# Attention operands split into high and low parts during the projection, head groups in the order B, C, A, and a full fp32 value product in group C

## The reference

```
h  = rmsnorm(x); z = h @ w_in                      # queries, keys, values of all three groups
A: 8 heads of 64, 2 key/value heads; q, k: rmsnorm per head, then a rotation (rope)
B: 4 heads; q = rmsnorm(cq) @ w_uq (64 + 32 rotated), k, v = rmsnorm(ckv) @ w_ukv,
   plus a rotated key kr of 32 that the four heads share
C: 4 heads with two maps of width 32 each: p_i = softmax(q_i k_i / sqrt(32) - slope * |distance|)
   a = p_0 - lam * p_1;  o = rmsnorm(a @ v)
x = x + concat(A, B, C) @ w_out
u = conv3(rmsnorm(x) @ w_up);  x = x + (silu(gate) * value) @ w_down        # width 2816
```

## Time and profile before

| | us |
|---|---|
| median of 3 runs | 3411.35 (3408.97 to 3412.27) |
| the profiled execution, its own time | 3407.34 |
| its span (first to last instruction) | 3405.5, mean granted clock 0.951 |
| PE busy in the span | 3034.8 (89%) |
| DVE, ACT, POOL busy | 2210.5 (65%), 1399.9 (41%), 825.5 (24%) |
| projection, layer 0 | from 42.8 to the first scores at 297.0 |
| attention, first transposes to the last unit | 310.7 to 857.8 |

### The profile page before, as it was taken

One profiled execution on the slowest core, in us unless ns is written; L12 is line 12 of the kernel. 1 busy time (PEld: TensorE's weight loads), 2 busy tenths in 40 slices (PEclk: granted clock), 3 DMA queues, 4 the chain that ended last, 5 costly groups with the idle time before them and its releaser, 6 DMA issues.

```text
span 3405.5 us, 41293 instructions
## 1 busy us (share of the span) xinstructions
PE 3034.8 (89%) x13488; PEld 2378.8 (70%) x13488; DVE 2210.5 (65%) x2575; ACT 1399.9 (41%) x1917; POOL 825.5 (24%) x472
## 2 busy tenths in 40 slices
PE   6888999666899999999889889995669999999996
PEld 5666777444678888888767667763447788888885
DVE  4863877899345656556567378779972556555555
ACT  3214888666232222222222178886643222222213
POOL 3113554653320000000121145555524100000002
PEclk8999999888999999999999999997789999999998
DMA  4323211210212112111133331111121112111112
GB/s 159 87 81 90 53 46 41 56 39 6 99 50 62 50 37 62 37 49 37 37 103 92 89 85 46 41 54 44 28 75 50 58 42 62 37 49 49 50 37 62
DMA packets 233562, 198.55 MB, mean 58 GB/s; under 512 B 49344, under 2 KB 207808, under 8 KB 233408
## 3 DMA queue, kind: packets, MB, share of 16 engines
q1 hardware_dynamic: 233408, 196.66, 20.1%
HBM read 163.07 MB, written 33.55 MB: 58 GB/s over the span
## 4 chain that ended last, share of the span: by engine, by line
PE 63%; DVE 15%; issue 13%; ACT 4%; DMA 2%; POOL 2%; DVEq 1%; ACTq 0%; SPq 0%; POOLq 0%
PE ps L1528 26%; PE ps L1542 13%; PE ps L1319 9%; PE ps L1417 5%; PE ps L1448 4%; DVE ps L1136 2%; DVE ptl L1178 2%; PE ps L1428 2%; PE ps L1429 2%; DVE r L1079 2%; PE ps L1513 1%; ACT prob L861 1%; PE ps L1460 1%; DVE rinv L1153 1%; ACT pth L891 1%
## 5 line engine op out<-in xcount | busy, mean ns | idle before, releaser
L574 POOL TENSOR_TENSOR w0l<-wraw,w0h 128x1024 fp32r<-128x1024 f32 x34 | 89.4, 2634 | 1692.7 <-ACT w0h L754 1692.7
L1448 PEld LDWEIGHTS ps<-cst,prob 128*128 128x128 f32 x2048 | 257.2, 148 | 272.2 <-DVE ptl L1178 141.9
L1448 PE MATMUL ps<-cst,prob 128*128 128x128 f32 x2048 | 336.3, 289 | 120.9 <-DVE ptl L1178 57.7
L1178 DVE TENSOR_TENSOR ptl<-ps,pth 128x512 fp32r<-128x512 f32 x512 | 349.0, 687 | 142.7 <-ACT pth L891 136.9
L1417 PE MATMUL ps<-stack 128*128 128x512 f32 (+1 forms) x1152 | 350.1, 426 | 96.6 <-ACT prob L861 77.0
L861 ACT ACTIVATE prob<-ps,nmx 128x1024 f32<-128x1024 f32 x320 | 356.7, 1115 | 83.7 <-DVE nmx L1140 63.6
L1257 DVE TENSOR_TENSOR xT<-ps,xT 128x512 f32<-128x512 f32 x352 | 242.4, 691 | 226.2 <-PE ps L1542 226.1
L891 ACT ACTIVATE pth<-ps 128x512 fp32r<-128x512 f32 x512 | 298.8, 595 | 192.6 <-PE ps L1448 188.7
L1417 PEld LDWEIGHTS ps<-stack 128*128 128x128 f32 (+1 forms) x1152 | 216.2, 199 | 180.9 <-ACT prob L861 115.4
L1319 PE MATMUL ps<-xgh,w0h 128*128 128x512 f32 x768 | 254.9, 414 | 49.9 <-DVE z L1049 15.1
L1542 PE MATMUL ps<-ah,dnh 128*128 128x512 f32 x704 | 276.3, 393 | 21.0 <-DVE dnl L1250 20.1
(11 more groups left out here) (183 smaller groups left out, 6088.1 us busy)
## 6 DMA issues: line engine op xcount, KB each, us to landing
wraw<-in_w_up SPq DMA_DIRECT2D x88, 512.0 KB, 4.6
draw<-in_w_down SPq DMA_DIRECT2D x22, 1024.0 KB, 5.0
wraw<-in_w_in SPq DMA_DIRECT2D x36, 512.0 KB, 4.5
x_d<-xT SPq DMA_DIRECT2D x2, 4096.0 KB, 15.8
raw<-qa_d SPq DMA_DIRECT2D x32, 256.0 KB, 3.8
raw<-ka_d SPq DMA_DIRECT2D x32, 256.0 KB, 4.2
vraw<-v_d SPq DMA_DIRECT2D x32, 256.0 KB, 3.1
wraw<-in_w_out SPq DMA_DIRECT2D x16, 512.0 KB, 5.0
```

Of the source, the lines that this page charges most:

```text
L1178: dve.tensor_tensor(ptl[:, s % NPT, :], ps[:, 4 + s % 2, :], pth[:, s % NPT, :].bitcast(F32), ALU.subtract).then_inc(pt_lo, 1)
L1448: ins = pe.transpose(ps[:, 4 + s % 2, m * P:(m + 1) * P], prob[:, b, m, s * P:(s + 1) * P], ident)
```

## The change

The stores of the projection now write high and low parts. After each tile or job ACT copies the high part into a ring of four slots (`hi_event`), DVE subtracts to get the low part (`lo_event`), and SP stores both (`store_event`); a ring slot pair is used again two events later, when its stores have landed (`ring_free`). A `z` slot is free with the low part. The DRAM arrays of A, B and C's operands and of A and B's values get a leading axis of two; C's values stay plain fp32. Attention loads the stacks directly (`load_operands`, `load_values`); `hi_operand`, `lo_operand`, `hi_values` and `lo_values` are gone, and so are the buffers `raw` and `vraw`.

The tiles alternate C and A, with A's key as tile 13. `uq` becomes three jobs of 128 rows (one of them all rotated parts, so there is one rotation in place of four; the host orders the columns of `w_uq`), and `tr` two jobs of 128 in place of four. The heads run in the order B, C, A; the units of B and C and one of A's are written out, and the loop runs over A. The operands of heads 0 and 1 are loaded during the projection, at tile 9.

In C the value product is one fp32 matmul a step (`vfull` with `ptf`) in place of the pair, `ptl` falls away, ACT copies the transposed probabilities unrounded, and DVE's `sum_output` scales the result itself; `copy_part` (ACT) and `scale_output` (POOL) do nothing there.

At the end of the FFN the last down weights go to slots of the up weights, so they can be split before group 9 is done; all 16 products of group 9 come after the last up products, and DVE interleaves its additions with taps, gate and splits (`last_step`).

```diff
-TILES += [("aq", A_Q + P * i) for i in range(4)] + [("ak", A_K)]
-TILES += [("cq_", C_Q), ("cq_", C_Q + P), ("ck_", C_K), ("ck_", C_K + P)]
-TILES += [("v", A_V), ("v", C_V), ("v", C_V + P)]
+TILES += [("cq_", C_Q), ("aq", A_Q), ("ck_", C_K), ("aq", A_Q + P), ("cq_", C_Q + P), ("aq", A_Q + 2 * P), ("ck_", C_K + P), ("aq", A_Q + 3 * P)]
+TILES += [("vc", C_V), ("ak", A_K), ("vc", C_V + P), ("va", A_V)]
...
-JOBS = {0: [("sx", 0)], 2: [("scq", 0)], 3: [("sckv", 0)], 4: [("uq", h) for h in range(4)],
-        5: [("sa", 4), ("ukv", 0), ("ukv", 1), ("tr", 0), ("ukv", 2), ("tr", 1), ("ukv", 3), ("tr", 2), ("tr", 3)],
-        6: [("sa", 5)], 7: [("sa", 6)], 8: [("sa", 7)], 9: [("sa", 8)],
-        14: [("tv", 13)], 15: [("tv", 14), ("tv", 15)]}
...
+JOBS = {0: [("sx", 0)], 2: [("scq", 0)], 3: [("sckv", 0)], 4: [("uq", 0), ("uq", 1), ("uq", 2)], 5: [("ukv", 0), ("ukv", 1)],
+        6: [("sa", 5), ("ukv", 2), ("ukv", 3)], 7: [("tr", 0), ("tr", 1)], 8: [("sa", 7)], 10: [("sa", 9)], 12: [("sa", 11)],
+        13: [("tv", 12)], 14: [("sa", 13)], 15: [("tv", 14), ("tv", 15)]}
...
+EVENTS = {4: [("z", 3), ("uq", 1), ("uq", 2), ("z", 4)], 5: [("uq", 0), ("ukv", 0), ("ukv", 1)], 6: [("z", 6), ("z", 5)], 7: [("tr", 0), ("tr", 1)],
+          8: [("z", 8), ("z", 7)], 10: [("z", 10), ("z", 9)], 12: [("z", 11)], 13: [("tv", 12)], 14: [("z", 13)], 15: [("tv", 14), ("tv", 15)]}
+EVENT_LIST = [e_ for t in range(NT) for e_ in EVENTS.get(t, [])]
+WHOLE = [("tv", 12), ("tv", 14)]
+SPLITS = [e_ for e_ in EVENT_LIST if e_ not in WHOLE]
...
-HEADS = [("A", h) for h in range(NA)] + [("B", h) for h in range(NB)] + [("C", h) for h in range(NC)]
+HEADS = [("B", h) for h in range(NB)] + [("C", h) for h in range(NC)] + [("A", h) for h in range(NA)]
...
+    qn_d, qr_d = dram("qn_d", (2, NB * NOPE, T)), dram("qr_d", (2, NB * ROPE, T))
+    kn_d, kr_d = dram("kn_d", (2, NB * NOPE, T)), dram("kr_d", (2, ROPE, T))
+    qc_d, kc_d = dram("qc_d", (2, NC * 2 * CQK, T)), dram("kc_d", (2, NC * 2 * CQK, T))
+    v_d, vc_d = dram("v_d", (2, T, (NKV + NB) * HD)), dram("vc_d", (T, NC * HD))
...
+                def store_event(kind, a):
...
+                    stored = ring_stored[n % 2]
+                    if (kind, a) in WHOLE:
...
+                    for s, ready in enumerate((split_hi, split_lo)):
+                        sp.wait_ge(ready, l * len(SPLITS) + split_no(kind, a))
+                        src = ring(kind, a, s).bitcast(F32)
...
+                            dst = {"aq": qa_d, "ak": ka_d, "cq_": qc_d, "ck_": kc_d}[name]
+                            sp.dma_start(dst[s, i * P:(i + 1) * P, :], src).then_inc(stored, 16)
...
+                def load_operands(hh):
+                    group, h = head(hh)
+                    st, full = stack[hh % 2], stack_full[hh % 2]
+                    if hh >= 2:
+                        sp.wait_ge(scores_done, l * NS + items_before(2 * hh - 2))
+                    if group == "A":
+                        for s in range(2):
...
                     else:
+                        for i in range(2):
+                            r0 = (2 * h + i) * CQK
+                            for c in range(4):
+                                rows = slice(c * CQK, (c + 1) * CQK)
+                                sp.dma_start(st[2 * i][rows, :].bitcast(F32), qc_d[c % 2, r0:r0 + CQK, :]).then_inc(full, 16)
+                                sp.dma_start(st[2 * i + 1][rows, :].bitcast(F32), kc_d[c // 2, r0:r0 + CQK, :]).then_inc(full, 16)
...
+                def load_values(hh):
+                    group, h = head(hh)
+                    full = v_full[hh % 2]
+                    if hh >= 2:
+                        sp.wait_ge(av_done, l * (8 * NU) + 16 * (hh - 1) + AV_CREDIT)
+                    if group == "C":
+                        sp.dma_start(vfull[hh % 2][:, :, :], vc_d.rearrange("(m p) c -> p m c", p=P)[:, :, h * HD:(h + 1) * HD]).then_inc(full, 16)
...
+                        load_operands(0)
+                        load_operands(1)
...
+                load_values(0)
+                load_values(1)
                 sp.dma_start(dtab[:, :], dist).then_inc(dtab_loaded, 16)
...
+                for hh in range(2, NB + NC + NA):
+                    load_operands(hh)
+                    load_values(hh)
...
-                def lo_operand(hh, i, s, h=None):
...
-                def hi_values(hh, h=None):
...
-                def lo_values(hh, h=None):
...
                 def scale_output(x):
...
+                    if x["group"] == "C":
+                        return
...
                 def pool_unit(x, prev, nx):
-                    hh, h = x["k"] // 2 + 1, x["hh"] + 1
-                    more = hh < NA + NB + NC
-                    ahead = operands_ahead(x)
-                    late = ahead and ahead[0] == "C"
                     diagonals(x)
-                    if ahead and not late:
-                        lo_operand(ahead[1], ahead[2], 0, ahead[3])
                     if nx and nx["group"] == "C":
                         mix_first(nx)
-                    if ahead:
-                        lo_operand(ahead[1], ahead[2], 0 if late else 1, ahead[3])
                     if prev:
                         scale_output(prev)
-                    if x["half"] == 1 and more:
-                        hi_values(hh, h)
-                    if late:
-                        lo_operand(ahead[1], ahead[2], 1, ahead[3])
-                    if x["half"] == 1 and more:
-                        lo_values(hh, h)
-                    if prev:
                         lo_mix(prev)
...
+                def ring_free(kind, a):
+                    n = event_no(kind, a)
+                    if n >= 2:
+                        act.wait_ge(ring_stored[n % 2], (l * RINGS[n % 2] + ring_dmas(n - 2)) * 16)
...
+                def hi_event(kind, a):
...
+                    act.activation(ring(kind, a, 0)[0:rows, :], src[0:rows, :], ACT.Copy).then_inc(split_hi, 1)
...
-                def hi_operand(hh, i, s, h=None):
...
                 def copy_part(x):
+                    if x["group"] == "C":
+                        return
...
-                        act.activation(pth[:, s % NPT, :], ps[:, 4 + s % 2, :], ACT.Copy).then_inc(pt_hi, 1)
+                        act.activation((ptf if x["group"] == "C" else pth)[:, s % NPT, :], ps[:, 4 + s % 2, :], ACT.Copy).then_inc(pt_hi, 1)
...
+                def lo_event(kind, a):
...
+                        src = e[:, 0, :] if kind == "uq" else z[:, a % 2, :]
+                        ins = dve.tensor_tensor(lo[0:rows, :], src[0:rows, :], hi[0:rows, :].bitcast(F32), ALU.subtract)
+                    ins.then_inc(split_lo, 1)
...
-                for h in range(NB):
-                    dve.wait_ge(job_free, l * NJ + job_no("uq", h) + 1)
-                    rope(e[:, h % 2, :], rb_, NOPE, 96, 8).then_inc(roped, 1)
-                    dve.wait_ge(roped, l * NB + h + 1)
+                for kind, a in EVENTS[4]:
+                    lo_event(kind, a)
+                dve.wait_ge(job_free, l * len(FREED) + free_no("uq", 0))
+                rope(e[:, 0, :], rb_, 0, P, 8).then_inc(roped, 1)
+                dve.wait_ge(roped, l + 1)
...
                 def sum_output(x):
-                    dve.wait_ge(part_copied, l * NU + x["u"] + 1)
+                    if x["group"] == "C":
+                        dve.wait_ge(av_done, l * (8 * NU) + x["u"] * 8 + 8 + AV_CREDIT)
+                        dve.wait_ge(norm_copied, l * NU + x["u"] + 1 + N_CREDIT)
+                        dve.wait_ge(mix_lo, l * NU + x["u"] + MIX_CREDIT)
+                        dve.tensor_tensor(osum[rows, :], ps[rows, 6 + x["half"], :], nrm[rows, :], ALU.mult).then_inc(o_ready, 1)
+                        return
...
-                        dve.wait_ge(pt_hi, l * (8 * NU) + x["u"] * 8 + s + 1)
-                        dve.tensor_tensor(ptl[:, s % NPT, :], ps[:, 4 + s % 2, :], pth[:, s % NPT, :].bitcast(F32), ALU.subtract).then_inc(pt_lo, 1)
+                        if x["group"] != "C":
+                            dve.wait_ge(pt_hi, l * (8 * NU) + x["u"] * 8 + s + 1)
+                            dve.tensor_tensor(ptl[:, s % NPT, :], ps[:, 4 + s % 2, :], pth[:, s % NPT, :].bitcast(F32), ALU.subtract).then_inc(pt_lo, 1)
...
+                def last_step(f, q):
+                    g = GROUPS - 2
+                    add_down(g, 0)
+                    outer_taps(f, 1)
+                    for j in range(1, 4):
+                        add_down(g, j)
+                    gate_value(f)
+                    for j in range(4, 6):
+                        add_down(g, j)
+                    lo_a(f, q)
+                    for j in range(6, 9):
+                        add_down(g, j)
+                    lo_down(GROUPS - 1)
+                    for j in range(9, 16):
+                        add_down(g, j)
...
-                            ins = three(outs, wqh[0:rows, k, a * 96:(a + 1) * 96], wql[0:rows, k, a * 96:(a + 1) * 96],
```

(32 more changed lines are left out.)

442 lines of the change are left out of this document (212 added, 230 removed).

## The result

| | before | after | forecast |
|---|---|---|---|
| median (us) | 3410.16 (4 runs of the same comparison) | 3257.31 (3254.08 to 3257.85, 4 runs) | 3240, range 3190 to 3290 |
| ratio to before | | 0.955 (95% interval 0.9538 to 0.9561) | |
| span of the profiled execution | 3405.5 | 3255.1 | 3234.7 (its sum of -170.8) |
| mean granted clock | 0.951 | 0.973 | |

The account below looks back on a forecast made before the run. PE was taken to bound A and B units, DVE C units. Attention −57.4, projection −17.3, `dtab` +1.3 and FFN end −12.0 give −85.4 us a layer, −170.8 in two: 3240 us, range 3190 to 3290.

Parts of the forecast that it names:

- A and B units: Attention units of groups A and B: PE sets the pace, so they stay at 12.9 and 14.4 us.
- C units: Attention units of group C: DVE sets the pace; 23.85 less 4.80 for `ptl` is 19.05, with POOL's share 20.4 us.
- 1.35 for POOL's work in VectorE's way: In a C unit, about a third of POOL's remaining 3.74 us was taken to delay DVE: 1.35 us.
- a sign of being wrong: In C, PE and DVE waiting for each other in turn, making a unit longer than either's own work; no size given.
- Rival 1: In C units, POOL's remaining work delays DVE in full: 22.8 us a unit, 3274 us in all; chance 0.13.
- The fp32 product: C's value product on PE: +0.31 us a step, 2.5 a unit, hidden by DVE, but only just.
- rival 4: The clock falls in C to 1.2 GHz: 33.6 us a unit, 3425 us in all, no gain; chance 0.02.
- Projection: Projection, a layer: waits −16.5, fewer `uq` jobs −3.1, clock −6.0, tail +8.3; sum −17.3 us.
- the tail of 8.3: End of the projection: A's key chain, last low part and longer store queue delay the first score by 8.3 us.
- The start of attention: Value loads ahead of `dtab` delay the first maximum by three issues of 0.43 us: +1.3 us a layer.
- End of the FFN: Last down products, a layer: PE's wait of 10.03 us goes, and 2.0 us at low clock; sum −12.0 us.
- rival 5: In attention, operands land late and PE waits for them; 8 us late a head gives 3464 us; chance 0.02.

Follow-up runs that it names:

- idle `ptl`: The changed kernel, with VectorE also making eight low parts a unit in group C that no product reads: 3288.46 us.
- The runs with less work for TensorE in C: The changed kernel with C's fp32 value product replaced by the split high and low pair (3290.07 us) or by one rounded product (3244.91 us).
- The two dtab runs: The changed kernel with the load of `dtab` issued ahead of the values (3241.64 us), or waited for only ahead of group C's first maximum (3243.43 us).
- both edits: The changed kernel with `dtab` issued ahead of the values and also waited for only ahead of group C's first maximum: 3240.49 us.

## Why the prediction was right, and where it was off

- **A and B units**: unchanged at 12.9 and 14.3 us, as predicted. PE is busy 95% and 97% of them.
- **C units**: 20.4 us predicted and measured, with a wrong composition. From 19.05 it went up by 1.35 for POOL's work in VectorE's way. L1165's 1285 ns show none. VectorE is busy 17.8 us a unit, not 19.05, and idle for the other 2.6, which was counted nowhere; where they come from is argued above (the order in which four queues wait for each other) and not shown. The idle `ptl` shows the slack from the other side: 4.3 us of VectorE's work cost 2.3. The number was right by luck, because these errors cancelled. The unit is longer than either engine's own work (PE 18.4, VectorE 17.8), which the prediction had named as a sign of being wrong.
- **Rival 1** (22.8 by the rule of the Trainium skill, SBUF — State Buffer, § Who interferes with whom) didn't come. The exclusion is in the trace all the same, on the other side: POOL's `lo_mix`, begun behind an L1165, has gone from 1375 ns to 2163, and VectorE keeps its 1285. The 1.35 was a share of POOL's time; what decides is which of the two starts first.
- **The fp32 product**: hidden in C, as predicted, with the wrong size: the term of 0.31 us a step is 0.45 for the product, and up to 0.2 more for the transposes. It shows at the seam from C to A, 32.5 us for two distances where 15.4 and 12.9 were counted, +4.2 us a layer. The last distance gives it back: there are six B distances where the sum has seven terms of 14.4, and one of 10.6 stands for the seventh. That too is luck. The sum of 31 distances is 476.7 us by forecast and by measurement; against before it is -56.4 and -55.9 where -57.4 was forecast, since the same distances were 533.1 and 532.6 there and not 534.1.
- **The clock** went up in C, from 0.80 to 1.00, the reverse of rival 4. The runs with less work for TensorE in C had 0.87 to 0.89.
- **Projection**: -34.8 against -34.6. In layer 0 PE's idle time fell by 8.7 us (16.5 less the tail of 8.3 counted) and its busy time by 10.4 (3.1 and 6.0 counted). How much of that is clock isn't shown; the mean is 0.95 before and after. Without the alternation 23.6 us of it are lost, by way of the weights' copies rather than the slots of `z`.
- **The start of attention**: this is the term that failed. The step "`load_values` of heads 0 and 1 now stand ahead of `dtab`: +1.3" had 0.43 us an issue and the landing of before. The four issues took 4.20 us and the landing 5.5 in place of 4.17, and what follows ran at the low clock. First scores to first transposes grew by 6.9 and 7.7 us, first scores to the first norm product by 8.9 and 9.6. The two dtab runs gave 15 to 17 us back, which is the miss.
- **End of the FFN**: from the second step's up products to the last down product it is -12.1 and -12.5 us, against -12.0. That is 24.6 in two layers, and the run that undoes it has 24.5 of it back in the same stretch; its timed 19.1 is within what the two intervals allow.
- **Late operands** (rival 5): within the units of layer 0 (300 to 790) PE waited for ScalarE's exponentials and VectorE's low parts, and for no load.

With `dtab` issued first, the forecast of 3240 would have been met: 3241.64; that version, or both edits with 3240.49, is the fastest of all here.

## What to carry to other kernels

A load that everything waits for is priced by its place in the queue and by what it shares the way with, not by the issue time of the loads put ahead of it; put it first, or wait for it where it is read. When the busiest engines in a stage are at 87 and 90%, neither sets the pace by itself. Put idle work in to see: what it costs less than its time is the slack that the engine had. Where two engines can shut each other out, look at who starts first; it costs nothing when the one that starts second has time to spare. A product that is hidden in one stage is paid at the seam to a stage that its engine bounds.

## What the runs showed of the hardware

- An fp32 product of 128x512 with 64 columns of weights takes 1.00 us in C at full clock, where one with 128 columns took 0.86 in a B unit.
- Four issues of value loads took 4.20 us after the projection's stores had landed, and the same queue had needed 1.71 us for four operand loads.
- Of two instructions that shut each other out (a mix of maps on VectorE, a subtraction on POOL), the one that began 0.16 to 0.31 us behind the other took 0.8 to 1.0 us longer. When they began within 0.03 us of each other, VectorE's took 1.1 us longer, in all 12 places.
- The granted clock of a C stretch was 1.00 with PE busy 90%, and 0.87 to 0.89 with PE busy 66 to 68%.
